# Splitting weights three pieces ahead of TensorE instead of four, in a four-layer fp32 block

## The reference

```
for layer in (1, 2):                      # first block
    x = x + mixer(rms_norm(x) @ w_in) @ w_out
x = rms_norm(x)
for layer in (3, 4):                      # second block
    x = x + rmsnorm(mixer(rmsnorm(x) @ w_in) @ w_out)
    gate, up = split(rmsnorm(x) @ w_gu)
    x = x + rmsnorm((silu(gate) * up) @ w_down)
```

## Time and profile before

| | |
|---|---|
| median of 3 runs | 3366.46 us |
| the profiled execution | 3364.88 us |
| its span, first to last instruction | 3363.1 us |
| TensorE busy | 3318.6 us (99%) |
| VectorE busy | 1984.3 us (59%) |
| ScalarE busy | 1570.3 us (47%) |
| mean granted TensorE clock | 0.998 |
| chain that ended last, TensorE's share | 94% |

### The profile page before, as it was taken

The page is one execution under the profiler, slowest core; times in us unless marked ns, Lnnn a source line. Parts: engine busy times, 40 slices in busy tenths (PEclk is TensorE's granted clock), DMA queues, the critical chain, the costliest instruction groups (busy, mean ns, idle before and its releaser), DMA issues.

```text
span 3363.1 us, 40637 instructions
## 1 busy us (share of the span) xinstructions
PE 3318.6 (99%) x16752; PEld 2802.4 (83%) x16752; DVE 1984.3 (59%) x2605; ACT 1570.3 (47%) x2166; POOL 59.8 (2%) x62
## 2 busy tenths in 40 slices
PE   9999999999999999999999999999999999999998
PEld 8888888888889888878888888888888788888887
DVE  5875665565766857664444444564667654444555
ACT  4573454454553545454444443453455544444443
POOL 0000000000001010000000000000000000000000
PEclk9999999999999999999999999999999999999999
DMA  6455445455443434455555555555323555555544
GB/s 255 163 197 197 166 146 198 163 200 186 179 164 126 150 126 160 152 180 186 193 193 196 192 188 188 183 209 183 135 99 116 199 186 185 194 186 200 189 177 160
DMA packets 83352, 592.50 MB, mean 176 GB/s; under 512 B 9248, under 2 KB 9760, under 8 KB 12512
## 3 DMA queue, kind: packets, MB, share of 16 engines
q1 hardware_dynamic: 80880, 576.24, 46.8%
q0 software_dynamic: 2288, 13.67, 1.1%
HBM read 587.77 MB, written 2.10 MB: 175 GB/s over the span
## 4 chain that ended last, share of the span: by engine, by line
PE 94%; DVE 3%; ACT 1%; issue 1%; DMA 0%; POOL 0%; SPq 0%; POOLq 0%; DVEq 0%; ACTq 0%
PE ps L2657 92%; DVE wlo L1470 1%; PE ps L3469 1%; DVE l L2287 0%; ACT whi L644 0%; PE ps L2807 0%; PE ps L3444 0%; ACT sq L654 0%; DVE xres L1752 0%; DVE xx L1606 0%; DVE l L1832 0%; DVE l L1833 0%; DMA col<-in_col 0%; PE ps L2897 0%; DVE xx L1493 0%
## 5 line engine op out<-in xcount | busy, mean ns | idle before, releaser
L1470 DVE TENSOR_TENSOR wlo<-raw,whi 128x1024 fp32r<-128x1024 f32 x1091 | 1309.9, 1220 | 880.1 <-ACT whi L644 878.9
L2657 PE MATMUL ps<-whi,xx 128*128 128x512 f32 x5184 | 1653.5, 394 | 7.4 <-DVE xx L1606 5.9
L644 ACT ACTIVATE whi<-raw 128x1024 fp32r<-128x1024 f32 x1091 | 1131.8, 1055 | 910.1 <-PE ps L2657 803.6
L2657 PEld LDWEIGHTS ps<-whi,xx 128*128 128x128 f32 x5184 | 974.4, 188 | 212.3 <-issue 7.7
L2657 PE MATMUL ps<-wlo,xx 128*128 128x512 f32 x2592 | 1010.1, 390 | 0.0
L2657 PE MATMUL ps<-xx,whi 128*128 128x512 f32 (+3 forms) x2464 | 781.5, 375 | 2.9 <-DVE xx L1493 2.7
L2657 PE MATMUL ps<-xx,wlo 128*128 128x256 f32 x2160 | 606.0, 281 | 0.0
L2657 PEld LDWEIGHTS ps<-wlo,xx 128*128 128x128 f32 x2592 | 487.8, 188 | 95.5
L2657 PEld LDWEIGHTS ps<-xx,whi 128*128 128x128 f32 (+2 forms) x2464 | 439.0, 186 | 88.4 <-DVE wlo L1470 3.5
L2657 PEld LDWEIGHTS ps<-xx,wlo 128*128 128x128 f32 x2160 | 404.7, 187 | 3.2 <-issue 1.9
L2657 PE MATMUL ps<-whi,fhh 128*128 128x512 f32 x704 | 274.7, 390 | 0.0
(11 more groups left out here) (355 smaller groups left out, 1686.0 us busy)
## 6 DMA issues: line engine op xcount, KB each, us to landing
raw<-in_ffn_gu SPq DMA_DIRECT2D x176, 1024.0 KB, 4.8
raw<-in_ffn_down SPq DMA_DIRECT2D x88, 1024.0 KB, 4.8
raw<-in_ab_in SPq DMA_DIRECT2D x64, 1024.0 KB, 4.8
raw<-in_ev_in SPq DMA_DIRECT2D x63, 1024.0 KB, 4.8
raw<-in_od_in SPq DMA_DIRECT2D x48, 1024.0 KB, 4.8
raw<-in_nsa_in SPq DMA_DIRECT2D x40, 1024.0 KB, 4.8
raw<-in_ev_out SPq DMA_DIRECT2D x16, 1024.0 KB, 4.7
raw<-in_od_out SPq DMA_DIRECT2D x16, 1024.0 KB, 4.8
```

The source lines that it names most:

```text
L644: self.e.activation(m.hi[i % NSPLIT][:, 0:w], m.raw[t % NRAW][:, off:off + w], ACT.Copy).then_inc(*self.up("hi", i))
L1470: self.e.tensor_tensor(m.lo[i % NSPLIT][:, 0:w], m.raw[t % NRAW][:, off:off + w], m.hi[i % NSPLIT][:, 0:w].bitcast(F32), SUB).then_inc(*se ...
L2657: return self.e.matmul(out, l, r, start=start, stop=stop, skip_group_check=True)
```

## The change

`ahead()` gets an argument and by default splits up to NSPLIT - 2 = 3 pieces beyond `used`. The two hand-written boundaries ask for NSPLIT - 1 = 4 as before. The number of buffers stays at 5.

```diff
-    def ahead(self):
+    def ahead(self, n=NSPLIT - 2):
 
-        while self.fed < min(self.used + NSPLIT - 1, len(self.m.pieces)):
+        while self.fed < min(self.used + n, len(self.m.pieces)):
             self.split(self.fed)
             self.fed += 1
@@ Scalar.boundary
-        self.ahead()
+        self.ahead(NSPLIT - 1)
         self.feed()
```

## The result

The changed kernel took 3387.23 us (median; 3386.59 to 3389.32) beside 3366.57 us for the kernel before on the same chip. The ratio is 1.0065, with an interval of 1.0053 to 1.0077: slower by 20.7 us. The prediction said 3378.7 us and a range up to 3384.5 us. The direction came as foretold, and TensorE waits for splits at the six places named; the size is 8.5 us above the forecast and 2.7 us above the range.

What follows compares the result with a forecast made beforehand. TensorE was taken as the bound, busy 3318.6 us, with splits as early as five buffers allow. Terms 2.3 + 2.2 + 2.7 + 2.7 + 1.8 + 0.5 = 12.2 us on 3366.46 gave 3378.7 us; range 3370.5 to 3384.5.

Steps and rivals of the forecast that it cites:

- the six places: Layer 1's end, layer 2's gates, layer 3 and 4 boundaries, f0's start, f1's first gates, layer 4's first block: 12.2 us.
- The reading by positions: Whole queue: every split's number drops by one, one split still precedes each step; steps gain 0, late splits cost time.
- Place 1: End of layer 1's recurrence: VectorE's split 2.3 us late, cost 2.3 us, covering a second such place 20 us on.
- the gates: Layer 2's gates: the first of five VectorE splits ends after TensorE's start of the piece before; cost 2.2 us.
- f1: First gate block of f1: the first of five VectorE splits comes late for the piece before; cost 1.8 us.
- f0: First pieces of f0: a split behind two squares on ScalarE comes 2.9 us late; cost 2.7 us.
- the boundaries: Boundaries of layers 3 and 4: the waiting piece starts 1.36 us later at each, together 2.7 us; f0's and f1's boundaries 0.
- I leave it out of the sum: Clock drops after new idle stretches at f0 and layer 2's gates, 1.7 us once or twice, counted only as a case.
- The clock falls too: Rival: half clock also at f0's first pieces, layer 2's gates or both, 3380.4 to 3382.1 us; chance 0.2.
- Half cost: Rival: backlogs begin one VectorE split (1.22 us) earlier, so the places cost 4.4 us, 3370.9 us; chance 0.13.
- the steps gain: Rival: TensorE's waits for softmax, decayed products and five more each shorten by 1.06 us, 3354.8 us; chance 0.06.
- nothing to measure: Rival: idle time of ScalarE and VectorE swallows the shift of one piece, 3366.5 us; chance 0.06.

Runs made afterwards that it cites:

- e1: Changed kernel with four pieces ahead restored in ten stretches of slots (some 140 of 1091), three elsewhere: 3366.92 us beside 3365.76 for the kernel before, ratio 1.0003.
- e4: Kernel before, with the split put behind the steps in five single slots (330, 398, 424, 775, 795): 3361.16 us beside 3365.76, ratio 0.9986.
- e2: Kernel before, with three pieces ahead only in slots 222 to 235 (layer 2's gates): 3368.5 us beside 3365.76, ratio 1.0009.
- e6: Kernel before, with three pieces ahead only in slots 828 to 841 (first gate block of f1): 3368.85 us beside 3366.08, ratio 1.0008.
- e12: Changed kernel with four pieces ahead restored in slots 0 to 15, 155 to 165 and 288 to 303: 3384.07 us beside 3365.39 for the kernel before, ratio 1.0057.
- e3: Changed kernel with overwritten matmuls filling TensorE's waits at pieces 228, 454 and 837: 3385.62 us beside 3365.76 for the kernel before, ratio 1.0059.
- e5: Kernel before, with three pieces ahead only in slots 0 to 15: 3367.38 us beside 3366.08, ratio 1.0005.
- e8: Kernel before, with the split behind the steps in runs of slots (330-332, 397-402, 423-430, 775-777, 794-798): 3360.13 us beside 3366.08, ratio 0.9982.
- e11: As e8, without slots 397 to 402 and with 421, 422 and 790 to 793 added: 3360.90 us beside 3365.39 for the kernel before, ratio 0.9986.
- e7: Kernel before, order unchanged, with overwritten matmuls filling its waits of 2.52 and 3.41 us: 3364.8 us beside 3366.08, ratio 0.9997.
- e9: Changed kernel, order kept, with overwritten matmuls filling its seven longest TensorE waits: 3381.56 us beside 3365.39 for the kernel before, ratio 1.0048.

## Why the prediction was right in kind and wrong in size

**The reading by positions was right.** The wait for the softmax stayed at 5.2 us, the split ahead of it was there under a lower number, and e1 shows no gain outside the places. e4 is the other half of the proof: as soon as the split really stands behind the steps, the softmax starts 1.93 us behind the eviction in place of 3.07, TensorE waits 2.27 us for it in place of 3.41, and the kernel gets faster. So the change doesn't let steps pass ahead of splits.

**The six places were right, and their sum a little small.** Forecast 12.2 us, measured without the clock 2.73 + 2.63 + 1.40 + 1.38 + 2.70 + 0.93 + 2.20 = 14.0. The lateness itself was well read (2.2 against a wait of 2.32; 1.8 against 1.90; 0.5 against 0.67). Place 1 is partly luck: half of its 2.73 us is lost at piece 58, at 190.85 us, some 17 us ahead of the place that the forecast named, and the named place itself (pieces 64 and 65) loses 1.45 us and not 2.3. The forecast had seen a second such place behind it and missed the one ahead. What the terms lacked is what a stop costs beyond its idle time: 2.62 for 2.32 us, 2.20 for 1.90, 0.93 for 0.67, 2.73 for three stops of 1.07, 0.41 and 0.47. That is 0.26 to 0.30 us for each new stop. (For the gates and f1 the cost is that of e2 and e6, where no half clock follows the same wait.) At f0 and at the boundaries TensorE had stopped before the change already, and there it cancels: 2.70 and 1.40 as forecast.

**Left out: places under 0.8 us and the start.** The step "two more places came out under 0.8 us each, and are left to the range" left out 0.43 and 0.93 us, and the start, taken as nothing, cost 1.06: two stops of 0.27 and 0.29 us with 0.25 us each beside. With 0.31 us more in layer 1 that is 2.7 us. Each is small; none was zero, and all had one sign.

**The step that failed: "I leave it out of the sum."** The clock was mis-sized. It was a case with a chance of 0.2 and a price of 1.7 or 3.4 us. In the traced execution it cost 1.60 us at the gates, 1.59 at f1 and 1.22 at the softmax, 4.4 us in the trace, and 20.7 - 16.2 = 4.5 us between the times of the changed kernel and of its filled version (two comparisons, so give or take some 6 us; the offsets are the sharper proof, though each is of one execution). The size of one stretch was right where TensorE is the only bound. The error was in where and whether. I had asked which single wait was long enough, and named those of 2.9 us at f0 and 2.2 us at the gates. At f0 it never came, behind 3.16 us, in either traced run that had that wait unfilled. It came behind 2.32 us at the gates and behind 1.90 at f1, which I had not named, and doubled at an unchanged 3.41 us. The changed kernel had five waits of 1.9 to 3.2 us more, each with a chance of a stretch (in the traced runs that had them, 6 of 14 were followed by one); five times 0.4 by 1.6 us, some 3 us, belonged in the sum, and more than two stretches in the range. This rate comes from the runs; the two stretches of the kernel before could not give it. So with first piece and rest: 14.0 + 2.7 + 4.4 + 0.55 = 21.7 of the 22.0 us of offset.

The clock is half of the miss of 8.5 us (20.7 - 12.2). The other half are the two paragraphs above it, 1.8 us in the terms and 2.7 us left out. With either half right the time would have come out at some 3382.7 us, inside the range; it took both to pass 3384.5. The reading "the two longest idle stretches of TensorE are 3.4 and 2.5 us" leaves out the start, where TensorE waits 5.5 us for `xres` and 2.7 us for `xx`; nothing in the sum hangs on it.

**The rivals.** *The clock falls too* was what happened, at other places and for more. *Half cost*, *the steps gain* and *nothing to measure* are each excluded: no backlog began earlier (the terms are above, not below, the forecast), no step gained, and the time rose by 0.65%.

## What to carry to other kernels

Write the queue out in order before trusting what an edit of a read-ahead depth is for: with one split per turn, one less ahead moves no split behind a step, it only gives each split's place to the piece before it, and costs where the next piece's split was already late. To let steps go first, swap them within the turn, and only at the turns where TensorE waits for a step; that gave 4.5 to 6 us here where the depth cost 21. How often a stop of 2 to 3 us is followed by half clock is known from 14 cases of one kernel only. In a kernel with TensorE at 98%, price each new stop at its idle time plus 0.3 us plus its share of a half-clock stretch of 1.6 us.

## What the runs showed of the hardware

**The same wait, with and without the clock's fall.** Waits of TensorE and the 3.4 us at half clock that begin in them or right behind, by traced run (one execution each):

```
wait, us                  half clock behind it in       none in
gates 2.32                changed                       e2, e12
f1 1.90                   changed, e12                  e6
boundary 3, 2.0           e12                           changed, e3
boundary 4, 2.0           e3, e12                       changed
f0 3.16                   -                             changed, e12
layer 3 2.52              before, changed, e1, e2, e3   e5, e6, e12
softmax 3.41, once        before, e1, e2, e12
softmax 3.41, twice       changed, e3, e5, e6
softmax 2.3               -                             e4, e8, e11
```

A stretch came with waits from 1.90 us on and stayed away at one of 3.16. With the long waits filled there was none ahead of the end (e7, e9). The Trainium skill (TensorE: Matmul & The Clock Gate, Part 1: The HAM clock gate) says that the half rate is the default and that activity lifts it. The trace agrees: every stretch ahead of the end begins in a wait of TensorE of 1.90 us or more, or at most 1.3 us behind one, and filling the waits takes the stretches away.

Which of two equal waits gets a stretch is not shown to depend on the version. How many stretches there are differs from one execution to the next of the same kernel, as the mean granted clock of each execution shows (number of executions, times in us):

```
                            0.997          0.998                     0.999
before, 33 executions       -              29, 3364.38 to 3367.64    4, 3363.77 to 3364.93
e2, 11 executions           1, 3370.35     9, 3367.74 to 3369.80     1, 3366.89
e6, 11 executions           -              10, 3367.97 to 3370.41    1, 3367.42
e7 and e9, 16 executions    -              -                         all
```

An estimate from the traces: two stretches of 3.41 us and the 5.05 us at half clock at the end (4.8 to 7.3 us in the traces) give the kernel before a mean of 0.9982, and one stretch less gives 0.9987. So the executions at 0.999 had one stretch less at least, and e2's slowest one more at least than the two in its trace. The traced execution of e2, without a stretch at the gates, may therefore be one draw of several, and so may that of the changed kernel with one; which waits the other executions had their stretches at can't be told, as each version has one trace. What a stretch costs is shown by the offsets around it; what sets it, no run here settles.

**A stop costs more than its idle time**, by 0.25 to 0.30 us, in eight places of the changed kernel. Its timeline at the gates shows where this comes from:

```profile
703.58 0.39 PE L2657 MATMUL ps<-wlo,xx 128*128 128x512 f32 x1
703.81 0.39 PE L2657 MATMUL ps<-whi,xx 128*128 128x512 f32 x1
706.52 0.50 PE L2657 MATMUL ps<-whi,xx 128*128 128x512 f32 x1 [2.32 <-DVE wlo L1470]
706.85 0.46 PE L2657 MATMUL ps<-wlo,xx 128*128 128x512 f32 x1
```

In an unbroken row these matmuls start 0.23 us apart, though each is shown to take 0.39 us. The last one ahead of the stop counts in full, 0.16 us more, and behind the first one the next starts after 0.33 us, 0.1 more: together some 0.27 us. (The ends of matmuls are modelled by the profile; the starts are enough for the sum.) Fillers don't save it: at piece 228 they left 0.28 us of idle time in e3 and 0.51 in e9, and the offset was 2.61 and 2.63 us, as with the bare wait (2.62), since the wait ends when VectorE has made the split, whatever TensorE does meanwhile.
